# Experts in units of 32 slots: four units in one block, in four column groups of TensorE, with copied weights

## The reference

```python
gidx   = top_1(softmax(x @ w_rg))              # one of 4 groups
e1, e2 = top_2(softmax(x @ w_re) in group gidx) # two of 8 experts of the group
for each expert e:                              # 32 experts
    xb  = tokens routed to e                    # n_e rows of 1024
    hid = silu(xb @ w_gate[e]) * (xb @ w_up[e]) # 1024 -> 256
    out[those tokens] += (hid @ w_down[e]) * gate_weight
```

## Time and profile before

| | us |
|---|---|
| three runs | 2381.4, 2384.69, 2386.16 (median 2384.69) |
| profiled execution | 2389.32 |
| its span, first to last instruction | 2387.5 |
| PE busy in the span | 2160.4 |
| DVE, ACT, POOL busy | 1216.1, 904.8, 475.9 |
| granted TensorE clock, mean | 0.958 of full |

### The profile page before, as it was taken

How to read it: one execution, slowest core, us unless ns; L and a number is a source line. 1 busy time by engine, 2 the same in 40 slices (tenths; PEclk the granted TensorE clock), 3 DMA queues, 4 the chain that set the end, 5 groups by cost and what they waited for, 6 DMA issues and landing times. The chain is left out here.

```text
span 2387.5 us, 33351 instructions
## 1 busy us (share of the span) xinstructions
PE 2160.4 (90%) x9900; PEld 1220.1 (51%) x9901; DVE 1216.1 (51%) x2408; ACT 904.8 (38%) x2111; POOL 475.9 (20%) x366
## 2 busy tenths in 40 slices
PE   5999999999999898897999998999939998999980
PEld 2666634444455446896777774555523333333320
DVE  4344356765345743555888776777642222222223
ACT  1333121111233311224779774434314434444434
POOL 0000033331111102344333110011121222222220
PEclk9999999999999998998999999999969999999995
DMA  8444113322356636885323324454546888888738
GB/s 345 151 150 159 66 65 112 141 89 88 102 184 231 195 128 191 267 272 201 98 85 107 103 93 157 162 149 153 202 160 207 268 276 315 279 280 300 205 76 299
DMA packets 182740, 424.45 MB, mean 178 GB/s; under 512 B 41513, under 2 KB 81321, under 8 KB 169721
## 3 DMA queue, kind: packets, MB, share of 16 engines
q1 hardware_dynamic: 159784, 352.33, 42.3%
q0 software_dynamic: 13472, 45.26, 8.1%
q10 hardware_dynamic: 9392, 25.74, 3.0%
HBM read 303.13 MB, written 124.85 MB: 179 GB/s over the span
## 5 line engine op out<-in xcount | busy, mean ns | idle before, releaser
L2352 PE MATMUL ps<-big,bias 128*64 x672 | 302.7, 604 | 2.9 <-DVE ex_wgu L2444 2.1
L2353 PE MATMUL ps<-ex_wgu,bias 128*64 128x512 f32 x672 | 302.7, 604 | 0.0
L345 PE MATMUL ps<-cp_wt,big 128*128 128x344 f32 x768 | 225.2, 453 | 0.0
L1870 PE MATMUL ps<-w_out,mo_yt 128*128 128x512 f32 x512 | 225.1, 597 | 0.0
L345 PEld LDWEIGHTS ps<-cp_wt,big 128*128 128x128 f32 x768 | 145.7, 191 | 76.8 <-issue 3.8
L1602 PE MATMUL ps<-at_v,at_pt 128*128 128x128 f32 (+1 forms) x1200 | 183.3, 291 | 0.5 <-DMA at_v<-v_d 0.5
L2352 PEld LDWEIGHTS ps<-big,bias 128*64 128x64 f32 x672 | 89.9, 139 | 182.2 <-issue 182.2
L1668 ACT ACTIVATE at_p<-at_p,at_low 128x256 f32<-128x256 f32 (+1 forms) x384 | 174.0, 456 | 19.1 <-DVE at_low L1631 18.8
L2403 ACT COPY ex_wgu<-big 128x4096 f32 x42 | 151.5, 3608 | 62.8 <-SPq L2273 31.8
L1602 PEld LDWEIGHTS ps<-at_v,at_pt 128*128 128x128 f32 x1200 | 149.5, 192 | 47.0 <-issue 36.4
L2364 PE MATMUL ps<-w_out,bias 128*64 x336 | 153.2, 598 | 2.6 <-DVE mod L2428 1.5
(11 more groups left out here) (349 smaller groups left out, 3716.1 us busy)
## 6 DMA issues: line engine op xcount, KB each, us to landing
big<-in_w_gate_up SPq DMA_DIRECT2D x32, 2048.0 KB, 11.2
w_out<-in_w_down SPq DMA_DIRECT2D x32, 1024.0 KB, 5.7
cp_w<-in_w_ada SPq DMA_DIRECT2D x24, 1024.0 KB, 5.2
ch_d<-pc_cv SPq DMA_DIRECT2D x20, 1024.0 KB, 4.3
at_v<-v_d SPq DMA_DIRECT2D x27, 512.0 KB, 3.9
o_d<-at_o SPq DMA_DIRECT2D x48, 264.0 KB, 2.1
mo<-o_d SPq DMA_DIRECT2D x16, 792.0 KB
pc_qkv<-ch_d SPq DMA_DIRECT2D x16, 768.0 KB, 5.4
```

The costliest lines, as they stand in the source:

```text
L345: last = nc.tensor.matmul(ps[:, ROW_A + g, 0:THIRD], m.ht[:, k, t * P:(t + 1) * P], wt[:, k, g * THIRD:(g + 1) * THIRD], start=(k == 0), s ...
L1870: last = nc.tensor.matmul(ps[:, 2 + 2 * b + n, :], yt[:, b, k, :], w[:, k, n * BANK:(n + 1) * BANK], start=(k == 0), stop=(k == KD - 1))
L2352: nc.tensor.matmul(ps[0:HB, 2 + b, :], xt[:, b, k, 0:HB], wgu[:, bass.ds(at * WGU + k * 2 * DE, 2 * DE)], start=(k == 0), stop=(k == KD - 1))
L2353: last = nc.tensor.matmul(ps[HB:P, 2 + b, :], xt[:, b, k, HB:P], wgu2[:, b, k, :], start=(k == 0), stop=(k == KD - 1))
```

## The change

Units are of 32 slots, four to a block (UN = 4). The four units of a block go to the four column groups of PE, 32 PSUM partitions each. Unit 0 reads its weights where they lie; those of units 1, 2 and 3 are copied to one fixed place (`wgu2` with three parts, no double buffer), in two halves by k: ACT copies unit 1, DVE units 2 and 3. The first half for block t+1 waits for the middle of gate_up(t) (`gu_half`), the second for its end. The down weights of units 1 and 2 (ACT) and 3 (DVE) are copied into space left in other tensors, also with one buffer. `xt`, `sg`, `hid` and `hidt` lose their second buffer. `arrived`, `gu_loaded` and `d_loaded` are gone: ACT and DVE wait on each of the four buffers' own DMA semaphores, with a count that they work out from `started` (`loads_of`), and PE waits for their copies alone. An expert of one unit with another of one unit among the three before it gets a second, empty unit (`near`). The router's tables get four columns in place of two, and the lists are gathered by four indirect DMAs in place of two.

```diff
-HB = P // 2
-NBLK = (2 * T // HB + NE) // 2
+UN = 4
+HB = P // UN
+NBLK = (2 * T // HB + 2 * NE) // UN
...
-                for n in range(2):
-                    pool.indirect_dma_start(out=lists[:, n * HB:(n + 1) * HB, :].rearrange("p s x -> p (s x)"), out_offset=None, in_=m.list_d.rearrange("r (n s) x -> (r n) (s x)", n=2),
+                for n in range(UN):
+                    pool.indirect_dma_start(out=lists[:, n * HB:(n + 1) * HB, :].rearrange("p s x -> p (s x)"), out_offset=None, in_=m.list_d.rearrange("r (n s) x -> (r n) (s x)", n=UN),
...
+                link(V.tensor_scalar(lone[:, 3:], pad[:, :], 1.0, None, ALU.is_le))
+                link(V.tensor_tensor(near[:, :], lone[:, 0:NE], lone[:, 1:NE + 1], ALU.add))
+                link(V.tensor_tensor(near[:, :], near[:, :], lone[:, 2:NE + 2], ALU.add))
+                link(V.scalar_tensor_tensor(near[:, :], near[:, :], 1.0, lone[:, 3:], ALU.min, ALU.mult))
+                link(V.tensor_tensor(pad[:, :], pad[:, :], near[:, :], ALU.add))
...
+        def started(eng, t):
+
+            return eng.value_load(m.by_block[0:1, 0, bass.ds(t, 1)], min_val=1, max_val=NE)
+
+        def at(eng, t, u):
+            return eng.value_load(m.by_block[0:1, 1 + u, bass.ds(t, 1)], min_val=0, max_val=NWB - 1)
+
+        def loads_of(b, experts):
+
+            return ((experts + (NWB - 1 - b)) >> 2) - 1
...
-                        arrived((b - 1) % NWB, i + (1 if b else 0), i + (1 if b else 0))
...
-                def gate_up(b, q, started, at):
-                    pe.wait_ge(*gu_loaded.n(started))
+                def gate_up(t, b, q, slot):
                     pe.wait_ge(*xt_ready[b].n(q + 1))
                     pe.wait_ge(*hid_ready[b].n(q))
-                    pe.wait_ge(*wgu2_ready[b].n(q + 1))
                     for k in range(KD):
-                        nc.tensor.matmul(ps[0:HB, 2 + b, :], xt[:, b, k, 0:HB], wgu[:, bass.ds(at * WGU + k * 2 * DE, 2 * DE)], start=(k == 0), stop=(k == KD - 1))
-                        last = nc.tensor.matmul(ps[HB:P, 2 + b, :], xt[:, b, k, HB:P], wgu2[:, b, k, :], start=(k == 0), stop=(k == KD - 1))
+                        if k % (KD // 2) == 0:
+                            pe.wait_ge(*gu_by_act.n(t * 2 + (1 + k // (KD // 2))))
+                            pe.wait_ge(*gu_by_dve.n(t * 2 + (1 + k // (KD // 2))))
+                        nc.tensor.matmul(ps[0:HB, 2 + b, :], xt[:, k, 0:HB], wgu[:, bass.ds(slot * WGU + k * 2 * DE, 2 * DE)], start=(k == 0), stop=(k == KD - 1))
+                        for u in range(1, UN):
+                            last = nc.tensor.matmul(ps[u * HB:(u + 1) * HB, 2 + b, :], xt[:, k, u * HB:(u + 1) * HB], wgu2[:, u - 1, k * 2 * DE:(k + 1) * 2 * DE], start=(k == 0), stop=(k == KD - 1))
+                        if k == KD // 2 - 1:
+                            last.then_inc(*gu_half.inc)
                     last.then_inc(*gu_done.inc)
...
             @block.scalar
+                for t, b, q, head, tail in blocks(act):
+                    if b:
+                        weights = weights_of(t)
+                    if not tail:
+                        next_weights = weights_of(t + 1)
+                        copy_gate_up(t + 1, 0, next_weights)
                     act.wait_ge(*gu_done.n(t + 1))
+                    b1, q1 = before(b, q)
+                    act.wait_ge(*hid_ready[b1].n(q1 + 1))
+                    nc.scalar.activation(sg[:, :], ps[:, 2 + b, 0:DE], ACT.Silu).then_inc(*sg_ready[b].inc)
                     if not tail:
                         take_x(t + 1, *after(b, q))
+                        copy_gate_up(t + 1, 1, next_weights)
                     act.wait_ge(*ht_done[b].n(q + 1))
+                    act.wait_ge(*y_done.n(t))
+                    nc.scalar.copy(hidt[:, :, :].rearrange("p k n -> p (k n)"), ps[:, 4, 0:DE]).then_inc(*ht_ready[b].inc)
+                    copy_down(t, weights)
...
             @block.vector
+                def copy_gate_up(t, h, weights):
+
+                    half = WGU // 2
+                    if h:
+                        dve.wait_ge(*gu_done.n(t))
+                    else:
+                        for b in range(NWB):
+                            dve.wait_ge(*wgu_in[b].n(loads_of(b, weights[0])))
+                        dve.wait_ge(*gu_half.n(t))
+                    for u in (2, 3):
+                        ins = nc.vector.tensor_copy(wgu2[:, u - 1, h * half:(h + 1) * half], wgu[:, bass.ds(weights[u - 1] * WGU + h * half, half)])
+                    ins.then_inc(*gu_by_dve.inc)
...
                 for t, b, q, head, tail in blocks(dve):
+                    if b:
+                        weights = weights_of(t)
+                    if not tail:
+                        next_weights = weights_of(t + 1)
+                        copy_gate_up(t + 1, 0, next_weights)
                     dve.wait_ge(*gu_done.n(t + 1))
                     dve.wait_ge(*sg_ready[b].n(q + 1))
...
                     if not tail:
+                        copy_gate_up(t + 1, 1, next_weights)
                         dve.wait_ge(xg_in[b], q * 16 + 16)
                         take_idx(t + 2, b)
                     if not head:
                         take_y(t - 1, *before(b, q))
+                    copy_down(t, weights)
```

More of the change, by code:

```diff
@@ L2269, in _ @@
             def _(sp):
-                def arrived(b, gu, down):
-                    sp.wait_ge(*wgu_in[b].n(gu))
-                    sp.sem_inc(*gu_loaded.inc)
-                    sp.wait_ge(*wd_in[b].n(down))
-                    sp.sem_inc(*d_loaded.inc)
                 def load_down(e, b):
                     sp.dma_start(wd[:, b * WD:(b + 1) * WD].rearrange("p (k n) -> p k n", k=DE // P), one(a["w_down"], e)).then_inc(*wd_in[b].inc)
-                for b in range(NWB - 1):
-                    arrived(b, 0, 0)
                 with sp.Fori(0, NE // NWB - 1) as i:
@@ L2293, in _ @@
                         load_down(e, b)
-                arrived(NWB - 1, NE // NWB - 1, NE // NWB - 1)
             @block.gpsimd
@@ L2382, in _ @@
                     for k in range(DE // P):
-                        last = nc.tensor.transpose(ps[:, 4, k * P:(k + 1) * P], hid[:, b, k * P:(k + 1) * P], m.ident)
+                        last = nc.tensor.transpose(ps[:, 4, k * P:(k + 1) * P], hid[:, k * P:(k + 1) * P], m.ident)
                     last.then_inc(*ht_done[b].inc)
                     if not tail:
-                        gate_up(*after(b, q), *next_weights)
-                down(1, q, *weights_of(t))
+                        gate_up(t + 1, *after(b, q), next_slot)
+                down(t, 1, q, at(pe, t, 0))
             @block.scalar
@@ new lines, in copy_down @@
+                def copy_down(t, weights):
+                    for b in range(NWB):
+                        act.wait_ge(*wd_in[b].n(loads_of(b, weights[0])))
+                    act.wait_ge(*y_done.n(t))
+                    nc.scalar.copy(m.mod[:, 2 * D:4 * D], wd[:, bass.ds(weights[1] * WD, WD)])
+                    for k in range(DE // P):
+                        ins = nc.scalar.copy(wd2[1][k], wd[:, bass.ds(weights[2] * WD + k * D, D)])
+                    ins.then_inc(*d_by_act.inc)
@@ L2411, in _ @@
                     if not tail:
                         take_x(t + 1, *after(b, q))
+                        copy_gate_up(t + 1, 1, next_weights)
                     act.wait_ge(*ht_done[b].n(q + 1))
-                    if not is_tile(t, 0) and not is_tile(t, 1):
-                        act.wait_ge(*y_done.n(t - 1))
-                    nc.scalar.copy(hidt[:, b, :, :].rearrange("p k n -> p (k n)"), ps[:, 4, 0:DE]).then_inc(*ht_ready[b].inc)
+                    act.wait_ge(*y_done.n(t))
+                    nc.scalar.copy(hidt[:, :, :].rearrange("p k n -> p (k n)"), ps[:, 4, 0:DE]).then_inc(*ht_ready[b].inc)
@@ new lines, in copy_down @@
+                def copy_down(t, weights):
+                    for b in range(NWB):
+                        dve.wait_ge(*wd_in[b].n(loads_of(b, weights[0])))
+                    dve.wait_ge(*y_done.n(t))
+                    nc.vector.tensor_copy(m.bias[:, spare:spare + WD], wd[:, bass.ds(weights[2] * WD, WD)]).then_inc(*d_by_dve.inc)
+                weights = weights_of(0)
+                copy_gate_up(0, 0, weights)
+                copy_gate_up(0, 1, weights)
+                for t, b, q, head, tail in blocks(dve):
+                    if b:
[3 more added lines that the diff above has]
+                        copy_gate_up(t + 1, 0, next_weights)
```

143 lines of the change are left out of this document (66 added, 77 removed).

## The result

The changed kernel took 2421.95 us, the median of four runs (2420.12 to 2426.84), beside 2385.43 for the kernel before (2381.4 to 2388.37, four runs): ratio 1.0158, 95% interval 1.0144 to 1.0172, 36.5 us slower. The profiled execution took 2426.84, the longest of the four; its span is 2425.0 beside 2387.5 before. The spans differ by 37.5, and this is what the profile must account for.

A forecast was written before the change was run, and what follows sets the result against it. The prediction took PE and the DMA engines, both close to full in the expert stage, as the bound. Its terms, -48.0 - 23.5 + 44.1 + 5.4 + 10 + 20 + 4.7, gave +12.7 and 2397 us, range 2358 to 2434.

The forecast's parts named there:

- Blocks and their pace: Expert stage: 38 blocks in place of 42, each still 12.0 us, -48.0 us.
- The rival of column groups that don't overlap: PE's four column groups run as two pairs in the expert stage: up to 2389 + 391 us; chance 0.05.
- The weights come late: Expert loads land too late for gate_up of blocks 4, 12, 13, 14, 16, 26 and 28: +44.1 us.
- block 13's part: Expert 13's load, queued at SP behind w_down 11, gate_up 12 and w_down 12, makes block 13 10.4 us late.
- The five blocks that I had at 3.9 each: Blocks 4, 12, 16, 26 and 28, whose gate_up load stands behind its predecessor's w_down: 19.5 us in all.
- The clock: PE's low clock behind the two long weight pauses: +5.4 us, up to 7 x 2.7.
- Gathers: Gathers issued later behind DVE's copies and register loads delay turn_x, eight odd blocks by 2 us: +20, between 0 and 60.
- PE's reads: PE's two by_block register reads a block, both near gate_up's end: +10 us, between nothing and 48.
- Ahead of the stage: Two more list gathers, and the first block's half copies, register load and computed waits: +4.7 us, bounds 2 to 7.
- `arrived` is gone, so the 13.3 us wait goes: ACT's longest wait for SP in the expert stage vanishes with the announcing, part of -23.5 us of stalls.
- Rival C: DVE's queue sets the pace, hid or gather 2.5 us late in every odd block: 2422 us; chance 0.22.
- Rival B: Expert weights land 9.3 us after issue, queued deeper, and gathers stay hidden: -18.6, 2366 us; chance 0.28.

The follow-up runs named there:

- The experiment with SP's order: The changed kernel with gate_up of expert e+1 issued ahead of w_down of expert e in SP's queue: 2379.7 us, ratio 0.9966.
- Without loads: The changed kernel without the weight loads of experts 4 to 31, the four buffers never refilled; one execution: 2340.51 us.
- the one with late reads: The changed kernel with gate_up ahead of w_down, gather indices ahead of the second half copies, and PE's register reads behind turn_x and down: 2359.16 us, ratio 0.9886.
- the last version: The changed kernel with gate_up ahead of w_down, gather indices as DVE's first act of an iteration, and PE's reads late: 2349.21 us, ratio 0.9842.

## Why the prediction was off

The direction held, late weights ate what fewer blocks gave, and 2422 lies in the range; the size was a third of what came: +12.7 on the profiled execution against +37.5. The step that failed is the price of PE's pauses: the low clock behind them was put at 5.4 behind the weights and at nothing behind the gathers, and it measured 15.4 and 12.7. The end of the stage had no term.

1. **Blocks and their pace**: right, 38 of 11.97. The rival of column groups that don't overlap is gone.
2. **"The weights come late"**: right in each of seven places and in the sum (42.3 for 44.1), though not in each term: block 13's part was 6.0 for 10.4. Its load was issued at E(12)+0.4 and landed 9.1 later, where my queue had it start at E(12)+1.4 and take 10.4, and 1.7 of the wait is counted with a late gather ahead of it. The five blocks that I had at 3.9 each took 3.9 to 5.4, 22.5 for 19.5. That the sum is within 2 us is in part luck. The experiment with SP's order shows the cause.
3. **The clock was the mis-sized term**: "After the two long pauses the clock falls, 2 x 2.7 = 5.4 (up to 7 x 2.7)". It fell behind all seven, at 1.2 to 2.8 each, 15.4: near the upper bound that I had written and not taken. I had one pause of 6.5 us in the rows and treated those of 4 us as too short, with no row that said so. They were not: behind a pause of 3.9 us gate_up took 9.50. The two long pauses that the 5.4 stood for, ahead of blocks 13 and 14, cost 3.0 together, less than any other two.
4. **Gathers were the other**: "20, between 0 and 60" measured 35.5. The waits alone were 22.8, near my number; I had no term for the low clock behind them, 12.7. I had the issue 0.6 us too late in even blocks (E+4.9 for 4.2 to 4.3) and 1.3 to 2.1 in odd ones (E+7.1 for 5.0 to 5.8), and the 10.5 us landing beside a load wrong (I took 6.0, the median). The errors partly cancel. The scatter I had wrong in sign: I expected more of the long ones of rows 12, and the median went from 2.29 us to 1.75.
5. **PE's reads**: 6.9 for 10. Without loads they show at 14.3, so the 10 lies between the two; that half the reads would cost about what all had cost was a guess that no row carried.
6. **Ahead of the stage**: 3.8 for 4.7. One pair of profiles is weak here: over the ten kernels with the new planner the stage began at 1789.4 to 1796.2, mean 1792.7, over the four with the old at 1784.2 to 1790.9, mean 1788.1. The means differ by 4.6, which is what the term said.
7. **The end**: no term for it, 7.1. I had costed the single buffer for w_down in the steady block and never walked the last one: 3.2 of the 7.1 are these copies and 1.7 the slow matmuls behind them; 1.5 are PE's sequencer.
8. **"`arrived` is gone, so the 13.3 us wait goes"**: wrong as a reason. Taken out alone it saved 4 us and the pause stayed, one block on; the order of SP's loads was behind it. The sum did not suffer, because I counted the new kernel's late weights afresh.

Terms 3, 4 and 7 are 10.0 + 15.5 + 7.1 = 32.6 too little; 1, 2, 5 and 6 are 6.5 too much; the rest is the 1.3 of the table. Rival C named the right time, 2422, for a cause that holds by half: the seven late gathers do all stand in odd blocks, where DVE's queue issues them latest, but they are 7 of 18, three of them behind a late hid, and without the loads PE waits 0.4 us for one of them; `hid` was never late by DVE's queue itself. Rival B failed on its condition, a landing of 9.3: the median was 11.5.

What stays open is how much each pause costs in clock. In the kernel with SP's order alone a turn_x that started 3.45 us behind E kept its clock,
```profile
2178.00:2182.00 4.00, 4.00 (x39) 1.42 (x37) 0.00 (x0) 2.81 (x2) 0.97 (x1) 1.00 1.05 328
```
and in the one with late reads 2.5 us behind E was followed by
```profile
2089.10:2091.10 2.00, 2.00 (x12) 1.67 (x16) 0.91 (x1) 0.00 (x1) 1.03 (x1) 0.50 1.07 334
2091.10:2093.10 2.00, 2.00 (x16) 0.48 (x20) 0.00 (x0) 2.00 (x2) 0.00 (x0) 0.65 0.98 256
```
so the length of a pause alone does not settle it. Nor was it traced to one transfer why block 13 waits 7.4 us in some versions and 9.5 in others, with expert 13's load issued at E(12)+0.45 in all.

## What to carry to other kernels

When a change packs more weights into a block, walk every expert through the load queue, and look at what each issue stands behind: here one order, w_down ahead of the next gate_up, cost 42 us, more than the 36.5 by which the change came out slower. Price a pause of PE with the slow matmuls behind it: in the changed kernel 13 of the 14 pauses, from 2.1 us on, cost another 1.4 to 3.1 us so, and the one of 1.7 us nothing. In the versions with edits some of 2.3 to 3.3 us cost nothing either, so this is a bound and not a price for each. Edits that speed one of two queues that feed the same instruction can show nothing until the other is done too; and walk the first and the last block, where nothing covers a copy.

## What the runs showed of the hardware

- Four column groups of 32 ran at the pace of two of 64: 6.89 and 6.92 us for 16 rounds of gate_up.
- A gather of 512 KB took 4.2 us alone and up to 10.7 beside the weights in the changed kernel; in the last version, which issues them ahead of E, the median is 9.4 against 4.5, and that of gate_up loads 12.7 against 11.5.
- PE's register reads and the addresses worked out from them cost 14.3 us in 38 blocks where nothing hides them, 0.2 to 0.7 a block; moved behind turn_x, the reads left delays of 1.0 us in all.
- The scatter's time on POOL grew with the DVE copy beside it: in the kernel before it took 1.6 us with no copy beside it and 2.3 beside 0.8 us of one, as in rows 12. Its median fell from 2.29 us to 1.75 in the changed kernel, where DVE's register loads come first and only 0.3 us of the copy lies beside most scatters. The Trainium skill (SBUF — State Buffer, Who interferes with whom) names the port that the two share.
